# The second feed-forward block by seven half products instead of eight, with its weight sums on GpSimd

## The reference, cut to what matters

```python
def swiglu(h, w_in, w_out):                       # h (tokens, 1024), w_in (1024, 5632), w_out (2816, 1024)
    gate, up = jnp.split(h @ w_in, 2, axis=-1)
    return (jax.nn.silu(gate) * up) @ w_out
...
    x_lat = x_lat + g2_l * swiglu(rmsnorm(x_lat, norm_w[i, 1]) * (1 + sc2_l) + sh2_l,
                                  ffn_w_in[i], ffn_w_out[i])
...
return rmsnorm(x_lat, final_norm_w)
```

## Time and profile before

| | us |
|---|---|
| median of 3 runs | 2135.62 (2132.86 to 2136.80) |
| the profiled execution | 2137.63 |
| its span | 2135.9 |
| PE busy in it | 2056.2 (96%) |
| DVE / ACT / POOL busy | 1273.0 / 869.9 / 79.8 |

### The profile page before, as it was taken

The page is one execution under the profiler, slowest core; times in us unless marked ns, Lnnn a source line. Parts: engine busy times, 40 slices in busy tenths (PEclk is TensorE's granted clock), DMA queues, the critical chain, the costliest instruction groups (busy, mean ns, idle before and its releaser), DMA issues.

```text
span 2135.9 us, 33524 instructions
## 1 busy us (share of the span) xinstructions
PE 2056.2 (96%) x12727; PEld 1816.3 (85%) x12742; DVE 1273.0 (60%) x1959; ACT 869.9 (41%) x1427; POOL 79.8 (4%) x127
## 2 busy tenths in 40 slices
PE   6999999999999999999999999999998999999998
PEld 3899999998889999999998877777875788888887
DVE  6656555567365774764765767777777543333334
ACT  3544333345232332332433555748384335232222
POOL 1000000000001000000000100000000000000000
PEclk8999999999989999999999999999999999999999
DMA  8422222233322443432332221211216222333332
GB/s 279 158 88 62 82 88 87 63 90 109 119 86 82 123 122 90 120 113 77 107 95 63 80 69 40 71 58 50 88 49 236 60 79 86 99 94 96 99 99 79
DMA packets 297916, 204.69 MB, mean 96 GB/s; under 512 B 5396, under 2 KB 289421, under 8 KB 296013
## 3 DMA queue, kind: packets, MB, share of 16 engines
q1 hardware_dynamic: 294349, 180.04, 28.6%
q0 software_dynamic: 3456, 23.09, 2.9%
HBM read 189.47 MB, written 13.63 MB: 95 GB/s over the span
## 4 chain that ended last, share of the span: by engine, by line
PE 82%; DVE 8%; ACT 5%; issue 2%; DMA 1%; SPq 0%; ACTq 0%; POOL 0%; DVEq 0%; POOLq 0%
PE G L327 56%; PE G L1211 12%; ACT e L1942 1%; PE S L2080 1%; PE S L839 1%; DVE acc L2111 1%; PE S L2076 1%; PE S L810 1%; PE S L450 1%; DVE wlo L314 1%; DMA adalo<-in_ada_w_dram 1%; ACT whi L310 1%; DVE hn L711 1%; DVE hlo L720 1%; PE G L434 1%
## 5 line engine op out<-in xcount | busy, mean ns | idle before, releaser
L327 PE MATMUL G<-hhi,whi 128*128 128x384 f32 (+2 forms) x1760 | 575.8, 378 | 28.9 <-DVE hlo L720 20.0
L314 DVE TENSOR_TENSOR wlo<-raw,whi 128x1024 fp32r<-128x1024 f32 (+2 forms) x213 | 248.1, 1165 | 483.7 <-ACT whi L310 483.5
L327 PE MATMUL G<-hhi,wlo 128*128 128x384 f32 (+2 forms) x1760 | 533.4, 353 | 0.0
L327 PE MATMUL G<-hlo,whi 128*128 128x384 f32 (+2 forms) x1760 | 532.9, 353 | 0.0
L310 ACT ACTIVATE whi<-raw 128x1024 fp32r<-128x1024 f32 (+2 forms) x213 | 216.1, 1014 | 730.8 <-PE G L327 479.5
L327 PEld LDWEIGHTS G<-hhi,whi 128*128 128x128 f32 x1760 | 320.1, 191 | 94.9 <-issue 40.1
L327 PEld LDWEIGHTS G<-hhi,wlo 128*128 128x128 f32 x1760 | 328.2, 191 | 20.1
L327 PEld LDWEIGHTS G<-hlo,whi 128*128 128x128 f32 x1760 | 328.3, 191 | 17.7
L327 PE MATMUL G<-mhi,whi 128*128 128x384 f32 (+2 forms) x544 | 163.6, 349 | 2.0 <-issue 0.9
L327 PE MATMUL G<-mhi,wlo 128*128 128x384 f32 (+2 forms) x544 | 162.6, 347 | 0.0
L327 PE MATMUL G<-mlo,whi 128*128 128x384 f32 (+2 forms) x544 | 162.5, 347 | 0.0
(11 more groups left out here) (352 smaller groups left out, 2984.5 us busy)
## 6 DMA issues: line engine op xcount, KB each, us to landing
raw<-in_ffn_w_in_dram SPq DMA_DIRECT2D x52, 512.0 KB, 3.9
raw<-in_ssm_w_in_dram SPq DMA_DIRECT2D x41, 512.0 KB, 4.0
raw<-in_hg_w_in_dram SPq DMA_DIRECT2D x40, 512.0 KB, 4.0
adaw<-in_ada_w_dram SPq DMA_DIRECT2D x20, 1024.0 KB, 5.4
adaf<-in_ada_w_dram SPq DMA_DIRECT2D x20, 1024.0 KB, 5.3
sraw<-in_ffn_w_in_dram SPq DMA_DIRECT2D x36, 512.0 KB, 5.1
raw<-in_ffn_w_out_dram SPq DMA_DIRECT2D x32, 384.0 KB, 3.6
raw<-in_ssm_w_out_dram SPq DMA_DIRECT2D x16, 512.0 KB, 4.1
```

The source lines that it names most:

```text
L314: dve.tensor_tensor(wlo[pn.slot][:, 0:kt, :], raw[pn.slot][:, 0:kt, :], f32(whi[pn.slot][:, 0:kt, :]), ALU.subtract).then_inc(s["lo"], 1)
L327: ins = pe.matmul(G[:, tl.slot, g0:g0 + n], w[pn.slot][:, k, :], r[:, k_base + k, t0:t0 + n], start=(first and k == 0 and i == 0), stop=(l ...
```

## The change

`PARTS` is now (4, 6, 6, 6) for both layers, and the functions of the first feed-forward take the layer `l`. The second feed-forward so has 4 classic blocks and 18 pairs, with halves of 256 tokens (`HALF`). In layer 1 five things are different from layer 0: the four weight sums are made by POOL (`ffn1_pool`); TensorE takes P2 before P3; ring slots and PSUM banks are exchanged, since panel numbers have the other parity; ACT takes the gate of the first half before that of the second; and the low splits stand in another order, the one of P5 waiting for the sum of P6, and the one of P6 for the sum of P3, because a sum and its low part share a place. Layer 0 keeps its instructions.

```diff
-PARTS = ((4, 6, 6, 6), (6, 8, 8))
+PARTS = (4, 6, 6, 6)
...
-        ON_TENSOR = (P1, P6, P5, P7, P3, P2, P4)
+        RING = ({P1: 0, P2: 1, P7: 2, P4: 3, P5: 4, P6: 5, P3: 6}, {P1: 2, P2: 3, P7: 0, P4: 1, P5: 4, P6: 5, P3: 6})
+        ON_TENSOR = ((P1, P6, P5, P7, P3, P2, P4), (P1, P6, P5, P7, P2, P3, P4))
+        BANKS = ({P1: 0, P2: 0, P6: 1, P5: 2, P3: 2, P7: 3, P4: 3}, {P1: 2, P2: 2, P6: 3, P5: 0, P3: 0, P7: 1, P4: 1})
+        FIRST_SPLITS = (P5, P6, P3, P1, P2, P7, P4)
+        HIGH = ((P1, P5, P6, P7, P3, P2, P4), (P1, P5, P6, P2, P7, P3, P4))
+        LOW = ((P1, P5, P6, P7, P3, P2, P4), (P1, P5, P2, P7, P6, P3, P4))
...
+        def sum_weights(eng, l, U, prod, first=None):
+            raw_in(eng, U)
+            ring_free(eng, l, U, prod, first)
             if prod in (P6, P3):
+                eng.wait_ge(s["ssm"], sum_count(U, P5 if prod == P6 else P6, first))
...
+            eng.tensor_tensor(sum_of(l, prod), a, b, op).then_inc(s["ssm"], 1)
...
+        def pair_lo(dve, l, U, prod, first=None):
+            dve.wait_ge(s["shi"], high(l, U, prod, first))
+            if l and prod in (P5, P6):
+                dve.wait_ge(s["ssm"], sum_count(U, P6 if prod == P5 else P3, first))
...
+            else:
+                high_of(P5, P6, P2)
+                gate_half(act, l, U, 0)
+                high_of(P7)
+                gate_half(act, l, U, 1)
+                mid_hi(act, l, U, j, 1)
+                high_of(P3, P4)
+            if not ahead:
+                act.wait_ge(s["spd"], ended(l, U, P2))
+                split_hi(act, downs, PAIRS)
...
+        def ffn1_pool(pool):
+            for p in (1, 2, 3):
+                def one(U, j):
+                    first = down_at(1, p - 1)[0] if isinstance(j, int) and j == 0 else None
+                    for prod in SUMS[first is None]:
+                        sum_weights(pool, 1, U, prod, first)
+                pairs_of(pool, 1, p, one)
```

More of the change, by code:

```diff
@@ L50 @@
 FFN = 2816
-PARTS = ((4, 6, 6, 6), (6, 8, 8))
+PARTS = (4, 6, 6, 6)
+assert sum(PARTS) * P == FFN
 PK = KT
-assert all(sum(p) * P == FFN and max(p) <= PK for p in PARTS)
-MB = max(PARTS[0])
+MB = max(PARTS)
 KH = KT // 2
@@ L1152, in ring_free, with high, low @@
             elif U.past(1):
-                eng.wait_ge(s["spd"], ended(U + (-1), prod))
-        def split_count(U, prod, first):
-            return U.n * 7 + (SPLITS[first is None].index(prod) + 1)
+                eng.wait_ge(s["spd"], ended(l, U + (-1), prod))
+        def high(l, U, prod, first):
+            return U.n * 7 + ((HIGH[l] if first is None else FIRST_SPLITS).index(prod) + 1)
+        def low(l, U, prod, first):
+            return U.n * 7 + ((LOW[l] if first is None else FIRST_SPLITS).index(prod) + 1)
@@ L1195, in pair_tensor, with bank_of @@
+        def bank_of(l, prod):
+            return Gq[:, BANKS[l][prod], 0:HALF[l]]
+        def pair_tensor(pe, l, U, first=None, between=None):
+            for prod in ON_TENSOR[l]:
+                pe.wait_ge(s["slo"], low(l, U, prod, first and first[0]))
                 if first is not None and prod in (P1, P5):
-                    last = first + (KT - 2 if prod == P1 else KT - 1)
+                    last = first[1] + (KT - 2 if prod == P1 else KT - 1)
                     pe.wait_ge(took[last.slot], last.turn + 1)
@@ L1575, in ffn1_tensor @@
-        def ffn1_tensor(pe):
-            def gate_up(pn, tl, i, cnt, ahead, p):
-                gate_up_tensor(pe, 1, pn, tl, LAT)
-            def begin(pn, tl):
-                product_pair(pe, 3, pn, tl, LAT)
-            def down(pn, tl, j, ahead, p):
-                product(pe, pn, tl, m["mhi1"], m["mlo1"], PARTS[1][p], LAT,
-                        need=lambda k: pe.wait_ge(s["mlo"], PARTS[0][0] + blocks_before(1, p) + k + 1))
-            def last(pn, tl):
-                product_ending(pe, 4, *ends(4)[0:2], m["mhi1"], m["mlo1"], PARTS[1][-1], LAT,
-                               need=lambda i, k: pe.wait_ge(s["mlo"], PARTS[0][0] + sum(PARTS[1])))
-            ffn1_loop(pe, gate_up, down, last, begin)
```

604 lines of the change are left out of this document (289 added, 315 removed).

## The result

| | time, us (median, lowest to highest) | profiled span, us |
|---|---|---|
| before | 2135.92 (2132.86 to 2137.31) | 2135.9 |
| changed | 2170.35 (2168.36 to 2175.89) | 2168.0 |

The ratio is 1.0166, 95% interval 1.0154 to 1.0178: 34.4 us slower, where the prediction had 9.8 and a range that ends at 2160. The direction was right, the size was not.

What follows compares the result with a forecast made beforehand. PE's matmul count and pace were taken to bound the second feed-forward. Products of -15.1 us and added waits and clock drops summed to +9.8 us on the 2135.62 median: 2145.4 us, range 2133 to 2160.

Steps and rivals of the forecast that it cites:

- products: Second feed-forward: a pair's 84 matmuls take 10.05 us against a classic block's 10.88, 18 times: -15.1 us.
- walk of a pair: Hand-overs inside parts: following PE, POOL and DVE from P6, the next P6 comes 0.47 us late, 15 times: +7.0 us.
- ends of parts: First down product after each part of pairs: PE waits 2.4 us for its panel's low part, three times: +7.2 us.
- first pairs: First pair of part 1: late weights, chained sums and low parts stall PE 4.8 us; parts 2 and 3 nothing.
- part 0: Down products after the classic blocks: +0.9 us for the last block's low part, +0.5 for two sums of h.
- clock: PE's granted clock drops behind stalls: 2.5 us after the 4.8 us stall, 0.5 each after three ends: +4.0 us.
- `product_ending`: End of the kernel: four steps fewer lie over the last norm's work: +0.5 us, bounds 0 and 1.4.
- the port decides: Rival for the pairs: POOL takes 1.3 us or more, or loses the port repeatedly; 2155 to 2160 us; 15%.
- transfers hide: Weight loads: a pair's 1 MB is issued some 8 us before it is needed and takes 5.1.
- the pace of the matmuls: PE in the second feed-forward: 0.2267 us per matmul of 512 columns, 0.1196 us per matmul of 256.

Runs made afterwards that it cites:

- e11: e9 with VectorE's sum for P7 replaced by a copy of one quarter of the weights, computation incomplete: 2126.41 us, 0.9959 of the kernel before.
- e1: Changed kernel with the first down panel's split moved up on ScalarE and VectorE at each end of a part: 2162.62 us, 1.0127 of the kernel before.
- e10: e9 with one of each pair's four sums, that for P7, made by GpSimd instead of VectorE: 2135.12 us, 0.9996 of the kernel before.
- e2: Changed kernel with all four weight sums of each pair moved from GpSimd to VectorE: 2147.70 us, 1.0052 of the kernel before.
- e3: Changed kernel with each first pair's weight transfer issued ahead of the last two down panels of the part before: 2158.77 us, 1.0105 of the kernel before.
- e4: Changed kernel with the edits of e1, e2 and e3 together: 2132.95 us, 0.9992 of the kernel before.
- e9: e4, first pairs' loads ahead of all down panels, their first three sums on GpSimd from the fourth down product, fourth combination's low part behind P7's: 2129.37 us.

## Why the prediction was wrong, step by step

| step | predicted, us | measured, us | from |
|---|---|---|---|
| products | -15.1 | -14.6 | e11: 10.07 in a pair that waits for nothing |
| walk of a pair, 15 times | +7.0 | +21.6 | 57.55 us for five hand-overs, 11.51 each |
| ends of parts, 3 times | +7.2 | +6.6 | 2.2 each; e1 takes them away |
| first pairs | +4.8 | +10.6 | 6.54, 2.01 and 2.01 |
| part 0 | +1.4 | +1.2 | 1.45 and 0.38, against 0.58 |
| clock | +4.0 | +8.3 | pitch behind six stalls, five with a drop |
| `product_ending` | +0.5 | +2.3 | last downs to the end of the span |
| sum | +9.8 | +36.0 of 37.3 | |

**The step that failed is the walk of a pair**: 0.47 us per hand-over were forecast and 1.44 measured. The walk leaves the trace at this sentence: "Now DVE's low part of P5, which waits for that sum, and POOL's sum for P7 both start: the split ends at 6.35, the sum, held up, at 7.4." In the pair shown above the sum did end at 7.4 (1969.27), but it was not held up. It held the split, which ended at 7.95. I gave the tie to VectorE without a reason. GpSimd goes on to its next instruction at once, VectorE learns of the result by a semaphore and is 0.07 to 0.15 us later, in all 15 hand-overs. P2's split, which the walk has ended at 7.9, ends at 9.6. From there on all is late: the low part of P7 ends at 10.6 (9.5 in the walk), that of P6 at 11.6 (10.4).

The order at the port is not the whole miss. Part 3's five hand-overs take 10.91, 11.45, 11.63, 11.85 and 11.71 us, where the walk has 10.52. This gives an estimate of the shares in the 14.6 us, with part 3 taken three times:

- Already the first, in which P2's split is not held, is 0.4 us above the walk. Its sums take 1.29 to 1.30 us where I took 1.17 (the upper bound of twice 0.61 was too low as well), and its splits of P5 and P7 are held. Over 15 hand-overs this is about 6 us.
- In the second P2's split loses as well. That is 0.45 us more, and 0.1 us comes from P6 itself, which starts slower when its weights are just in time: about 5.5 and 1 us over 12 hand-overs.
- In the last three GpSimd's first sum begins while VectorE is still at its last split of the pair before, and takes 1.47 to 1.75 us. The walk has no such hold: about 2.5 us in all.

How much the lost tie at P5 costs by itself is not shown. e10 suggests little, since there the next split paid when VectorE was first. The rival "the port decides" (11.2 us, 15%) was the case, with a price 0.3 us too low; of its two conditions the sums of 1.3 us just held, and it was VectorE that lost the port again and again. That the sums on GpSimd are the cause is shown by e2, which takes them away, and by e10, which puts a quarter of them back.

The Trainium skill, "SBUF — State Buffer", section "Who interferes with whom", calls this port an exclusive lock and says that issue order decides who blocks; that the first keeps it for the whole instruction, it says of VectorE's modes with two ports. The traces agree and show the same for operations with two inputs: GpSimd, first by 0.08 us, kept its 1.30 and VectorE stood for 1.1; in e10 VectorE was first by 0.02 us and kept its 0.68. I had cited the lock and left out the issue order.

**First pairs.** That in parts 2 and 3 "the weights land in time, nothing" was wrong: sums of 1.98 and 1.77 us and a held low part of P1 (2.31 for two) made 2.0 us each. In part 1 the weights came 2 us later than counted, because the landing of 5.1 us was reckoned from the issue as it is within parts; here the transfer was issued at 1813.1, 0.4 us behind a down panel, and was there at 1820.3, after 7.2. The working itself has a slip of 0.2 us (3.5 + 2.9 - 3.7 is 2.7, not 2.9). e3 shows that an early transfer removes all three; that "transfers hide" held within parts, where no pair waited for one, but not at the borders.

**The clock** took twice what I gave it: a drop came behind both kinds of stall, at 6.5 and at 2.0 to 2.2 us, five times out of six (the third first pair was spared), at 1.3 to 1.9 us each. The forecast had left it open for stalls of 2.4 us and taken 0.5 us for each. My 1.5 us for three ends should have been 5.3. In its cause it is part of the stalls: e1's gain of 11.5 is 6.6 of waits and 5 of clock.

**What held:** the pace of the matmuls, the three ends to within 0.2 us each, the wait for part 0's last low part (1.6 against the pace, as forecast; the view lists 1.45 of it). **`product_ending`** was outside its bounds; from e4, which has no clock drop there, 51.6 us from the last downs to the end, where before has 60.2 less 48 matmuls of 0.2267. No experiment took that apart, and it stays open. Nor is it known why the section begins up to 7 us earlier or later from program to program.

## What to carry to other kernels

Before work is moved to GpSimd, list what VectorE does at that moment: each operation with two inputs in SBUF waits for what is left of such an operation on GpSimd. Here VectorE was busy, its holds counted in, for about 10.1 us of a pair with the sums on GpSimd (34.58 of 40 us) and for 9.7 us with all four sums on itself (37.12 of 40 us at 10.45 us a pair): the move relieved it of nothing. Where two engines are released by the same event, walk the loop with either one first and keep both ends, and look at what stands right behind the winner, as in e10 that paid. If the moved form has a shorter cover at its borders, move the next stage's first split ahead of the last results. In this kernel the sums back on VectorE, that split and early weights turned 1.7% slower into a tie (e4), and the further edits at the start of part 1 into 0.4% faster (e9).

## What was not expected of the hardware

An addition of 512 columns on GpSimd takes 1.26 to 1.30 us, one of 256 0.61: between these two the duration goes with the columns, and a start-up can't be seen. They are only two sizes, and both inputs of the shorter one are one broadcast tile. A wait of 2.0 us brought the granted clock down to 0.50 in one first pair and not in the other, at the same place of two parts that are alike. A product that gets its weights just in time starts 0.1 us slower even where no wait is listed: P6 takes 1.54 us for its 12 matmuls there and 1.44 elsewhere.
